# A recurrent gate tile of one 96-channel head and a third of a fourth head, in a two-block network on one core

## The reference, cut to what matters

```
z = rms_norm(x) @ w_in + b_in;  xb and gb are 1536 columns each of z
v = causal_depthwise_conv(xb, conv_b_w, conv_b_b)              # 4 taps
r = sigmoid(block_diag(v, w_rg_a) + b_rg_a);  i = sigmoid(block_diag(v, w_rg_x) + b_rg_x)
log_a = -8 * r * softplus(-lam);  a = exp(log_a)
b = sqrt(1 - exp(2 log_a)) * i * v                              # the root is 1 at the first token
h[t] = a[t] * h[t-1] + b[t]
y_b = (h * gelu(gb)) @ w_b_out
```

## Time and profile before

| | |
|---|---|
| median of three runs | 2661.38 us |
| the profiled execution | 2662.28 us |
| its span, first to last instruction | 2660.5 us |
| TensorE busy | 2496.4 us, 94% |
| VectorE busy | 1412.4 us, 53% |
| ScalarE busy | 811.1 us, 30% |
| mean granted TensorE clock | 0.972 |

### The profile page before, as it was taken

The page is one execution under the profiler, slowest core; times in us unless marked ns, Lnnn a source line. Parts: engine busy times, 40 slices in busy tenths (PEclk is TensorE's granted clock), DMA queues, the critical chain, the costliest instruction groups (busy, mean ns, idle before and its releaser), DMA issues.

```text
span 2660.5 us, 26241 instructions
## 1 busy us (share of the span) xinstructions
PE 2496.4 (94%) x11144; PEld 2014.8 (76%) x11144; DVE 1412.4 (53%) x1699; ACT 811.1 (30%) x1202; POOL 2.8 (0%) x7
## 2 busy tenths in 40 slices
PE   7999999999999469999999999999789999999778
PEld 5686868688888248888888888888678777878567
DVE  5574655598899975243232232334565334631365
ACT  4434352522122162333022131221332232221354
POOL 0000000000000000000000000000000000000000
PEclk9999999999999789999999999999799999999889
DMA  3110202011111002311111111121112111111401
GB/s 125 35 51 25 62 20 64 18 54 56 48 48 40 24 1 63 91 46 55 51 47 53 48 48 48 48 64 48 48 41 60 40 32 42 46 48 48 135 12 68
DMA packets 224951, 133.15 MB, mean 50 GB/s; under 512 B 12730, under 2 KB 220858, under 8 KB 224834
## 3 DMA queue, kind: packets, MB, share of 16 engines
q1 hardware_dynamic: 224834, 131.47, 17.0%
HBM read 125.12 MB, written 6.32 MB: 49 GB/s over the span
## 4 chain that ended last, share of the span: by engine, by line
PE 81%; DVE 13%; ACT 4%; issue 1%; SPq 1%; DMA 1%; ACTq 0%; DVEq 0%
PE bank L534 24%; PE bank L536 24%; PE bank L535 24%; DVE uc L1534 4%; PE bank L601 4%; DVE sa L1534 2%; DVE wlo L1403 1%; PE bank L568 1%; DVE u_in L1534 1%; PE bank L762 1%; PE bank L778 1%; PE bank L670 1%; DVE tmp L1773 0%; DVE uc L1650 0%; PE bank L867 0%
## 5 line engine op out<-in xcount | busy, mean ns | idle before, releaser
L534 PE MATMUL bank<-h_hi,whi 128*128 128x512 f32 x2000 | 787.0, 394 | 3.6 <-issue 3.3
L536 PE MATMUL bank<-h_hi,wlo 128*128 128x512 f32 x2000 | 780.6, 390 | 0.0
L535 PE MATMUL bank<-h_lo,whi 128*128 128x512 f32 x2000 | 780.3, 390 | 0.0
L534 PEld LDWEIGHTS bank<-h_hi,whi 128*128 128x128 f32 x2000 | 376.9, 188 | 84.8 <-issue 5.4
L535 PEld LDWEIGHTS bank<-h_lo,whi 128*128 128x128 f32 x2000 | 376.8, 188 | 80.8 <-issue 2.9
L536 PEld LDWEIGHTS bank<-h_hi,wlo 128*128 128x128 f32 x2000 | 376.7, 188 | 79.0
L895 ACT ACTIVATE whi<-raw 128x1024 fp32r<-128x1024 f32 (+2 forms) x212 | 216.7, 1023 | 450.8 <-PE bank L536 447.0
L1403 DVE TENSOR_TENSOR wlo<-raw,whi 128x1024 fp32r<-128x1024 f32 (+2 forms) x212 | 251.2, 1185 | 174.5 <-ACT whi L895 173.1
L1534 DVE SCALAR_TENSOR_TENSOR uc<-u_in,par,uc 128x1024 f32<-128x1024 f32 x163 | 205.2, 1278 | 1.1
L536 PE MATMUL bank<-ff_hi,wlo 128*128 128x512 f32 x512 | 199.2, 389 | 0.0
L534 PE MATMUL bank<-ff_hi,whi 128*128 128x512 f32 x512 | 199.2, 389 | 0.0
(11 more groups left out here) (341 smaller groups left out, 3074.0 us busy)
## 6 DMA issues: line engine op xcount, KB each, us to landing
raw<-in_w_in SPq DMA_DIRECT2D x92, 512.0 KB, 3.7
raw<-in_w SPq DMA_DIRECT2D x64, 512.0 KB, 3.8
raw<-in_w_b_out SPq DMA_DIRECT2D x16, 384.0 KB, 3.0
raw<-in_w_out SPq DMA_DIRECT2D x11, 512.0 KB, 3.5
x_in<-in_x SPq DMA_DIRECT2D x8, 512.0 KB, 5.3
raw<-in_w_a_out SPq DMA_DIRECT2D x8, 512.0 KB, 3.8
raw<-in_w_o SPq DMA_DIRECT2D x8, 512.0 KB, 3.6
xcols<-in_x SPq DMA_DIRECT2D x16, 256.0 KB, 2.8
```

What stands on the lines that cost most here:

```text
L534: pe.matmul(target, lh, rh, start=start, stop=False, skip_group_check=True)
L535: pe.matmul(target, lh, rl, start=False, stop=False, skip_group_check=True)
L536: last = pe.matmul(target, ll, rh, start=False, stop=stop and point is not None, skip_group_check=True)
```

## The change

The channels of a group are dealt out differently. Tile t of a group holds on its partitions 0 to 95 the whole head t, and on partitions 96 to 127 the t-th third (32 channels, `PART`) of the group's fourth head. Columns of w_in, rows of w_b_out and all per-channel parameters of the branch are loaded in this order, so most of these loads are cut in two pieces of 96 and 32 channels (runs of 384 and 128 bytes in w_in). The 512 parameter rows are reordered, those of the branch last.

A head in a tile needs one 96 x 96 product per gate and half. The fourth head's input is put together in a tile of its own, `fourth`, by three copies of 32 partitions on ScalarE (`fourth_in`), after the last GELU of the group before; its four products stand on TensorE between the blocks gb 1 and gb 2; their tanh goes to `fourth_gate` (`fourth_gates`), and each gate tile copies its 32 partitions from there into T1 and T3. On ScalarE the tanh of the i gate moves from before exp to after the second tanh. In SyncE's order four x tiles instead of two go ahead of the first rows, and eight loads of single bias columns come after the rows; VectorE waits for them. GpSimd's clearing of the gate weights goes.

```diff
 PARAMS: the branch's b_in, conv_b_b, b_rg_a, b_rg_x, lam, conv_b_w now stand last
+GROUP_RNN, PART = 4 * HEAD, HEAD // 3
         def need_rnn(kind, col, g, t):
-            need((kind, g, t), w_in, 0, DT, col + (g * GT + t) * P, P)
+            number[kind, g, t] = len(blocks)
+            first, rest = col + g * GROUP_RNN + t * HEAD, col + g * GROUP_RNN + GT * HEAD + t * PART
+            rows_ = lambda c, n: w_in[:, c:c + n].rearrange("(k p) c -> p k c", p=P)
+            blocks.append(([(slice(0, P), (0, HEAD), rows_(first, HEAD)), (slice(0, P), (HEAD, P), rows_(rest, PART))], DT, P))
...
+        for name, column in [("b_in", Z_XB), ("b_in", Z_GB), *RNN_ROWS.items()]:
+            n = 4 * (TAPS_B if name == "conv_b_w" else 1)
...
+            for t in range(GT):
+                for c0, c1, source in ((0, HEAD, t * HEAD), (HEAD, P, GT * HEAD + t * PART)):
+                    done = 0
+                    while done < n:
+                        at_row = r + t + GT * done
+                        m = min(n - done, -(-(P - at_row % P) // GT))
...
             def load_gates(g):
-                for n in range(2):
-                    w.wait_ge(*at("gate_w_clear", n))
...
+                for n, name in enumerate(("w_rg_a", "w_rg_x")):
+                    w.wait_ge(*(at("gate", g - 1, 3, n, 1) if g else at("x", DT - 1, 1)))
+                    sp.dma_start(gate_w[n][:], A[name][0, 4 * g:4 * g + 4].rearrange("q r c -> r q c")).then_inc(
+                        *landed(f"gate{n}", ("gate_w", g, n)))
...
-            load_x(0)
-            load_x(1)
+            for t in range(4):
+                load_x(t)
             load_rows(0)
-            for t in range(2, NT):
+            for t in range(4, NT):
                 load_x(t)
             ahead(0)
             for s in range(1, 4):
                 load_rows(s)
+            for n, name in enumerate(("b_rg_a", "b_rg_x")):
+                for g in range(NG):
+                    first = g * GROUP_RNN + GT * HEAD
+                    sp.dma_start(fourth_bias[0:HEAD, 4 * n + g:4 * n + g + 1], A[name][:, first:first + HEAD].rearrange("l c -> c l")
+                                 ).then_inc(*landed("fourth_bias", ("fourth_raw", n, g)))
...
             def gate_tile(g, c):
-                rows_ = [a for a, cc in PAIRS if cc == c]
+                source, point = (v[c][0:HEAD, :], ("rnn_in", g, c)) if c < GT else (fourth[:], ("fourth", g, GT - 1))
                 for n in range(2):
                     w.wait_ge(*at("gate_w", g, n))
                     for half in range(2):
                         b = bank("gate", g, c, n, half)
-                        for m, a in enumerate(rows_):
-                            w.wait_ge(*at("rnn_in", g, a))
-                            last = pe.matmul(b[:], gate_w[n][:, PAIRS.index((a, c)), :], v[a][:, cut(half)], start=m == 0,
-                                             stop=m == len(rows_) - 1)
-                        last.then_inc(*up("pe_done", ("gate", g, c, n, half)))
+                        w.wait_ge(*at(*point))
+                        pe.matmul(b[0:HEAD, :], gate_w[n][:, c, :], source[:, cut(half)], start=True, stop=True).then_inc(
+                            *up("pe_done", ("gate", g, c, n, half)))
...
                 for t in range(1, GT):
                     block(("gb", g, t), h, "h")
+                    if t == 1:
+                        gate_tile(g, GT)
...
+            def fourth_in(g, t):
...
+                act.activation(fourth[t * PART:(t + 1) * PART, :], v[t][HEAD:P, :], ACT.Copy).then_inc(*did(("fourth", g, t)))
+
+            def fourth_gates(g):
+                for n in range(2):
+                    for half in range(2):
...
+                        act.activation(fourth_gate[n][:, cut(half)], bank("gate", g, GT, n, half)[0:HEAD, :], ACT.Tanh,
...
             def gate_tile(g, c):                       # ScalarE
...
+                w.wait_ge(*at("fourth_gate", g, 0, 1))
+                act.activation(T1[HEAD:P, :], fourth_gate[0][part, :], ACT.Copy).then_inc(*did(("fourth_moved", 0, j)))
+                w.wait_ge(*at("fourth_moved", 0, j))
                 act.activation(T2[:], T1[:], ACT.Exp, ...)
                 act.activation(T1[:], T1[:], ACT.Tanh, ...)
+                for half in range(2):                  # before: ahead of the exp, 128 partitions
...
+                    act.activation(T3[0:HEAD, cut(half)], bank("gate", g, c, 1, half)[0:HEAD, :], ACT.Tanh, ...)
+                act.activation(T3[HEAD:P, :], fourth_gate[1][part, :], ACT.Copy).then_inc(*did(("fourth_moved", 1, j)))
                 act.activation(T1[:], T1[:], ACT.Sqrt).then_inc(*did(("keep", j)))
...
             for g in range(NG):                        # ScalarE
                 for t in range(1, GT):
                     gb_tile(g, t)
+                    if t == 1:
+                        fourth_gates(g)
...
                     gb_tile(g + 1, 0)
+                    for t in range(GT):
+                        fourth_in(g + 1, t)
...
+            w.wait_ge(*at("fourth_raw", 1, NG - 1))    # VectorE, behind turn_rows(3)
+            dve.tensor_scalar(fourth_bias[0:HEAD, :], fourth_bias[0:HEAD, :], 0.5, None, ALU.mult).then_inc(*did(("fourth_bias",)))
...
-            for n in range(2):                         # GpSimd
-                pool.memset(gate_w[n][:], 0.0).then_inc(*up("pool_done", ("gate_w_clear", n)))
```

More of the change, by code:

```diff
@@ L272, in build_program @@
                 a.rearrange("(k p) -> k p", p=P) if len(a.shape) == 1 else a.rearrange("l t (k p) -> (l t k) p", p=P))
[L273 to L278, removed]
+            spans = [(0, rows)]
+            if name == "b_in":
+                spans = [(0, Z_XB // P), (Z_SA // P, rows)]
+            if name in RNN_ROWS:
+                spans = []
+            for done, last in spans:
+                while done < last:
+                    r = offsets[name] + done
+                    n = min(last - done, P - r % P)
+                    row_pieces[r // P].append((rows_in[r // P][r % P:r % P + n, :], flat_rows[done:done + n, :]))
+                    done += n
+        for name, column in [("b_in", Z_XB), ("b_in", Z_GB), *RNN_ROWS.items()]:
+            n = 4 * (TAPS_B if name == "conv_b_w" else 1)
+            a = A[name] if name != "conv_b_w" else A[name].rearrange("l m c -> l (m c)")
+            groups = a[0:1, column:column + n * GROUP_RNN].rearrange("l (g c) -> (l g) c", c=GROUP_RNN)
+            r = offsets[name] + column // P
+            for t in range(GT):
[4 more added lines that the diff above has]
+                        m = min(n - done, -(-(P - at_row % P) // GT))
+                        first = at_row % P
+                        row_pieces[at_row // P].append((rows_in[at_row // P][first:first + GT * (m - 1) + 1:GT, c0:c1],
+                                                        groups[done:done + m, source:source + c1 - c0]))
+                        done += m
         h = pair("h", "h", 0, DT)
@@ L288, in build_program @@
         T1, T2, T3 = (sb(f"lru{i}", "g", o + 4096 * i, [P, SEQ]) for i in range(3)); o += 3 * 4096
[L289 to L299, removed]
+        gate_w = [sb(f"gate_w{n}", "g", o + 1536 * n, [HEAD, 4, HEAD]) for n in range(2)]; o += 2 * 1536
+        fourth = sb("fourth", "g", o, [HEAD, SEQ]); o += 4096
+        fourth_gate = [sb(f"fourth_gate{n}", "g", o + 4096 * n, [HEAD, SEQ]) for n in range(2)]; o += 2 * 4096
+        fourth_bias = small[:, 180:188]
         EDGE = [0, 4224 + 16 * 4096]
@@ L1464, in xb_tile @@
                 if g:
-                    w.wait_ge(*at("gate", g - 1, 1 if t == 0 else 2, 1, 1))
+                    w.wait_ge(*at("gate", g - 1, t, 1, 1))
+                    w.wait_ge(*at("fourth", g - 1, t))
                 for m in range(TAPS_B):
```

76 lines of the change are left out of this document (44 added, 32 removed).

## The result

The changed kernel takes 2705.74 us (median of four runs, 2704.59 to 2707.79) against 2661.64 beside it: a ratio of 1.0165, 95% interval 1.0153 to 1.0177. Slower was forecast, but the size was not: +44.1 instead of +25.4, and 2705.7 lies above the range of 2670 to 2699. The profiled execution has a span of 2706.0 us and a mean granted clock of 0.958.

The account below looks back on a forecast made before the run. TensorE was taken to bound the four groups, VectorE's convolution the end of the stage. Start 6.0, first fourth head 3.4, three groups 12.9 and group 3 3.1 made +25.4 on 2661.4: 2687 us, range 2670 to 2699.

Parts of the forecast that it names:

- the start: Before the first block: 52 small parameter loads at 0.345 us each on SP delay the fourth tile's row transpose, +6.0 us.
- Rival (b): The parameter rows hide, so they cost 0 before the first block: 2681 us, chance 0.10.
- the banks: Ring of eight: TensorE stalls 5.9 us before xb 0 and 6.4 in gate 2, until VectorE frees a bank.
- (d): Ring does not hold TensorE, small copies cost 0.42 us; xb 0 starts before E+9 (E: gate products begin); 2647, chance 0.06.
- (e): Ring does not hold TensorE, but ScalarE's small copies cost their full time: 2667 us, chance 0.07.
- the fourth head's products: On TensorE between gb 1 and gb 2, where nothing waits: +3.44 us per group.
- the groups: Three groups of the recurrent stage, each 2.5 us longer plus 1.8 for the clock: +12.9 us.
- The clock: After stalls in a group TensorE resumes at 1.2 GHz: +1.8 us per group, bounds 0 and 3.4.
- (a): The same as the forecast but without the clock loss in the groups: -5.4, 2681 us, chance 0.18.
- ScalarE's copies: Two copies of 32 x 1024 per gate tile, 1.06 us each; with the moved tanh, +1.25 us on the chain per tile.
- Group 3: VectorE starts its taps 3.75 us later and splits va 2's weights late: +3.1 us, carried into the tap stage.
- rival (c): In w_in's loads, runs of 384 or 128 bytes take as long as 512: start 9.6 us, 2690 us, chance 0.12.

## Why the prediction was wrong, point by point

*The failed step: the start.* "SP spends 0.34 us on each" was read from issues of plain rows and given to pieces with a step of three partitions; these take 0.62. The count of 52 issues and the begin of the small loads (17.2 against 17.8) were right. Of the 52, 44 have the step: 38 of the fourth tile's 43, and six of b_in in the third tile. The upper bound, 0.45 each, was still below it: a bound had been set by a guess around the one kind of issue that the trace had, not by a row. With 0.62 for these the forecast's own sum would have been 17.8 + 8 x 0.345 + 44 x 0.62 = 47.8 for the end of the last issue, rows at 49.6 and +18.4 instead of +6.0: 2699. The plain rows show this term, -18.0 for its removal, and the two queues show that it could be hidden. Rival (b), that the rows hide, is the worst of the lot: they were the largest single loss.

*Right: the banks.* Stalls of 6.0 us (forecast 5.9) ahead of xb 0, and of 3.8 to 5.0 ahead of gate 2's third product. The latter was forecast as 6.4, without the half clock that stretches xb 0 in front of it: it takes 13.6 us in group 0 and 11.1 with the stalls filled. xb 0 starts at E+13.1, not before E+9, and twice the products cost 3.5 us instead of 41, so (d) and (e) are out.

*Right: the fourth head's products*, 3.4 us a group: measured as the row of 3.6 us for four, and when they were moved off the path, -13.2 for four groups.

*Right in kind, short in size: the groups*, 4.3 forecast and 5.4 measured. The second release came at 153.72 - 121.35 = 32.4 us behind the first gate product in all three groups, forecast 31.85. From there to the next fourth head's products TensorE waits for nothing and takes 82.2, 81.0 and 81.9 us; with the lengths that the same work has where the stalls are filled it would be 78.9. So the half clock costs 2.8 us a group on average where 1.8 was forecast, and without it a group would take 125.6, the forecast's 125.5. The clock is the term of this sum that was too small. The filled stalls gave back only 1.7 of it, because the ninth output product then waits for VectorE's copy until E+84.6; the prediction had that bank free at E+83.7, level with its use, and put nothing down for it. (a) is out.

*ScalarE's copies* cost 1.05 us with 32 partitions, as with 128, as the forecast took them. The kernel after:

```profile
134.80 1.05 ACT L1027 ACTIVATE lru<-fourth_gate 32x1024 f32<-32x1024 f32 x1
135.88 1.28 ACT L1029 ACT_TABLE_LOAD   x1
137.17 1.06 ACT L1029 ACTIVATE lru<-lru 128x1024 f32<-128x1024 f32 x1
```

*Group 3*, 3.1 forecast and 5.6 measured. VectorE's split of va 2's weights ends at 633.4 instead of 590.6, so 4.2 of it are VectorE's later clock (42.8 less 19.0, 3.4 and 16.2); then TensorE, which waited 2.0 us for it, has half clock for 3.4 us (from 634.9 to 638.3) and hands on the rest:

```profile
633.55 0.47 PE L558 MATMUL bank<-h_hi,whi 128*128 128x512 f32 x1 [2.02 <-DVE wlo L1458]
```

 That second part is read from the trace and was not tested by itself.

*Hidden, as said:* the gate weights, the narrow runs of w_in (the plain-row kernel still has them and starts at 31.7, so rival (c) with its 9.6 us at the start is out), the four tanh of the fourth head, and VectorE's wait for the bias columns, which ended at 55.5 instead of 41 and was covered because the rows came later too: ScalarE adds the first bias at 59.85.

## What to carry to other kernels

The price of a DMA issue is that of its form: look for a row with the same step over partitions before multiplying, and where there is none, set the bound from another kind of row or say that there is none. An engine whose work is made shorter gains nothing while a ring of banks ties it to another engine's chain: find the release that ends last, and ask what stands right behind it. Here it was a second limit 1.7 us below the first, and the shorter products paid only when the release, the chain and the place of the fourth head's products had all been mended.

## What the hardware showed unexpectedly

Issue time on SyncE's queue, from start to start: 0.34 us for rows to neighbouring partitions, also of 384 and 128 bytes; 0.44 where such a piece has 16 rows; 0.62 for 2 to 16 rows to every third partition. ScalarE's queue took the same 0.6 (1.81 us for three); while both queues issued such pieces, either took up to 0.8.

Around stalls of 4 to 6 us TensorE's granted clock was at 1.2 GHz for 6.8 us: behind the second stall of group 0 all of it fell on work, at the first it fell from 2.4 to 1.2 GHz at 133.1, 1.3 us before TensorE went on. Behind the 2.0 us stall at 633.55 it was at 1.2 GHz for 3.4 us. When repeated products filled the stalls of the groups it stayed at 2.4.

The table load of ScalarE takes 1.28 us and stands right ahead of the instruction that needs it, but not always behind its wait. Ahead of the recurrence gate's tanh, which waits for TensorE and for VectorE, it came behind the wait (146.77, idle 1.34 before). Ahead of the square root of the kernel before, which waits for VectorE alone, it came first, and the wait of 0.79 us followed it. What decides it was not tested. In the first case a tanh of one column (0.20 us) ahead of the wait took the load off the chain.
